# Hybrid decoder step on one core: in the u stage POOL makes the low part of the next u block before it asks for expert rows

## The chip, the core and the metric

The kernel runs on one core of a Trainium2 chip. Its time is the device time of one execution in microseconds (us), the median of several runs. The core has engines that run side by side, each with a queue of its own that it works through in order: PE multiplies matrices, DVE, ACT and POOL work on vectors, and SP issues DMA transfers. ACT and POOL issue DMAs too. The engines are kept in step by semaphores alone: an engine that waits stops everything behind the wait in its own queue.

## The reference, cut to what matters

One layer of a decoder for 512 prompt tokens and 8 x 4 sample tokens, D = 1024 wide. The change lies in its last part, PEER: a mixture of 16384 experts of one neuron each.

```
hn = rms_norm(h);  y = h + peer(hn)
peer: qh = xt @ w_pq; sub = qh . sub_keys;  top-16 per half -> 256 candidates -> top-16 (8 heads)
      pre = einsum('td,thkd->thk', xt, expert_u[experts]);  act = gelu(pre)
      out = einsum('thk,thkd->td', gate * act, expert_v[experts])
```

So each token picks 8 x 16 = 128 experts, takes the dot products of its row with their rows of expert_u, and adds up their rows of expert_v with the weights gate * gelu.

## The kernel before, in words

**Two ways to the experts.** 416 of the 544 tokens (DT) go the dense way: PE multiplies all 16384 rows of expert_u and later all rows of expert_v. The other 128 tokens (NG) go the sparse way: for each of their 128 picks POOL gathers one expert row per token by an indirect DMA (128 rows of 4 KB, `fetch`, L1721), and DVE takes the dot product (`dots`, L1731) or, in the last stage, the weighted sum (`weigh`, L1883). I call the gather with index m gather m and its dot product dot m; m runs from 0 to 127 for expert_u, and goes on from 128 for expert_v.

**The u stage.** expert_u is worked in 128 blocks of 128 experts; x counts pairs and s is 0 or 1, so block n = 2x + s, and I call the turn of the loop for (x, s) place n. A block goes through four engines: SP loads it (L1661), ACT rounds it to the high part u_hi (L1686) when PE is done with the block two before it, POOL subtracts to get the low part u_lo (`lo_u`, L1706), PE makes 24 matmuls with the two parts (`pre`, helper lines L2241 to L2243), ACT applies Gelu (L1702) and SP stores the result. u_hi and u_lo have two buffers each.

**What DVE does meanwhile.** First routing: for five groups of tokens it finds the top 16s (L1476 to L1544), 12 or 16 blocks of PE work beside each group (`WINDOW`), and PE turns each group's picks (L1308, L1313). Then the gate part: 104 quads of 4 tokens; for each, DVE builds one-hot matrices (L1558, L1561; at most 4 quads ahead, `HOT`), PE multiplies them (L1337), ACT copies them out (L1415). 13 quads make a gate block, and PE's four blocks of `pre` are cut into halves and spread between them. In both parts the dots stand inside DVE's code at fixed points: up to 13 in each routing group from the second on, 46 in the gate part, after every second quad. DVE waits there for the gathered rows.

**What sets the order around the change.** The tables `FETCH_X` say which gathers are asked for at which place; in the gate part they run two gathers ahead of the dots (`FETCH_LEAD`). In a routing group 13 gathers are spread over the places, at most one at most places. The gathered rows have 3 buffers in routing and 5 later, and `fetch` waits for the dot that frees its buffer. POOL's queue holds gathers and `lo_u` in one order, written by the loop in `pool_ffn`. `lo_u` for block n+1 waits for ACT's u_hi of that block, so for PE's end of block n-1. After the u stage comes the dense v stage, in which DVE, PE and POOL work on 128 blocks of expert_v (`lo_v` is L1911, DVE's product of gates and activations L1867, its low part L1873); its first two `lo_v` stand inside the last places of the u loop.

Of the kernel before, what the change touches and what calls it, by code (L numbers as in the profile page):

```python
# [167 lines left out]
def hybrid_step(nc, x_p, x_s, kc, vc, conv_state, s0, nmix, win, wg8, qkw, convw, alog, dtb, dnw, wout, nffn,  # L168
                wpq, skt, eu, eu_rows, ev, pos_t, lnc_p, lnc_s, squares,
                y_p, y_s, k_p, v_p, conv_out, s_p, k_s, v_s, s_s, gates_dram, acts_dram):  # L170
    with ExitStack() as ctx:
# [990 lines left out]
        def pool_sample(pool, chain):  # L1162
            pool_ffn(pool, chain)
# [26 lines left out]
        def raw(k):  # L1190
            return w_first if k == NW1 else w_raw[k % 2]
# [376 lines left out]
        def pool_ffn(pool, chain):  # L1568
            pool.wait_ge(kv_out, 16 * (NKV + 2))
            for k in range(NW1, NW3):  # L1570
                pool.wait_ge(w_hi_ready, k + 1)
                pool.wait_ge(w_used, k - 1)
                nc.gpsimd.tensor_tensor(out=w_lo[:, k % 2], in0=raw(k)[:], in1=w_hi[:, k % 2].bitcast(F32),
                                        op=ALU.subtract).then_inc(w_lo_ready, 1)
            pool.sem_inc(ff["gate_mm"], HOT)
            for s in range(2):
                pool.sem_inc(gate_out[s], 16)
                pool.sem_inc(act_out[s], 16)
            lo_u(pool, 0, 0)
            for x in range(XS):  # L1580
                for s in range(2):
                    for m in FETCH_X[2 * x + s]:
                        fetch(pool, m)
                    if s == 0 or x + 1 < XS:
                        lo_u(pool, x + s, 1 - s)
                if x in (FIRST_V, FIRST_V + 1):
                    lo_v(pool, x - FIRST_V)
            pool_dense(pool)
# [28 lines left out]
        XS = PK // 2  # L1617
# [86 lines left out]
        def lo_u(pool, x, s):  # L1704
            pool.wait_ge(dn["uhi"], 2 * x + (s + 1))
            nc.gpsimd.tensor_tensor(out=u_lo[s][:], in0=u_raw[2 * (x % 2) + s][:], in1=u_hi[s][:].bitcast(F32), op=ALU.subtract).then_inc(dn["ulo"], 1)  # L1706

        def fetch(pool, m):

            if m == 0:  # L1710
                few_wait(pool, "idx", 1)
            if m == DOT0[NT]:
                pool.wait_ge(ff["sub"], 4 * (NT - 1) + 1)
            last = ROW_LAST[m]
            if last is not None and last < PICKS:
                few_wait(pool, "dot", last + 1)
            elif last is not None:
                few_wait(pool, "sum", last - PICKS + 1)
            table = eu_rows if m < PICKS else ev.rearrange("a b d -> (a b) d")
            n = m % PICKS  # L1720
            nc.gpsimd.indirect_dma_start(out=rows_g[ROW_AT[m]][0:NG, :], out_offset=None, in_=table,  # L1721
                                         in_offset=bass.IndirectOffsetOnAxis(ap=idx_g[0:NG, n:n + 1], axis=0)).then_inc(row_in[ROW_AT[m]], 16)
# [186 lines left out]
        def lo_v(pool, f):  # L1909
            pool.wait_ge(dn["vhi"], f + 1)  # L1910
            nc.gpsimd.tensor_tensor(out=v_lo[f % 4][:], in0=v_raw[f % 4][:], in1=v_hi[f % 4][:].bitcast(F32),  # L1911
                                    op=ALU.subtract).then_inc(dn["vlo"], 1)

        def pool_dense(pool):
            for n in range(FETCH_LEAD):
                for m in FETCH_V[n]:
                    fetch(pool, m)
            for f in range(2, PK):
                for m in FETCH_V[f - 2 + FETCH_LEAD] if f - 2 + FETCH_LEAD < len(FETCH_V) else ():
                    fetch(pool, m)  # L1920
                lo_v(pool, f)
# [475 lines left out]
```

## Time and profile before

| | us |
|---|---|
| median of 3 runs (lowest, highest) | 2228.98 (2225.56, 2231.54) |
| the profiled execution, its own time | 2227.2 |
| its span, first to last instruction | 2225.4 |
| PE busy | 2014.9 (91%) |
| DVE busy | 1540.5 (69%) |
| POOL busy | 1158.6 (52%) |
| ACT busy | 771.4 (35%) |

Times in the profile run from the start of the span. The u stage runs from about 850 to 1635 us: routing to 1222, gates to 1480, then blocks without gates. The v stage runs from there to about 2216. Idle time of an engine is shown in square brackets behind the instruction that ended it, with what released it. The granted clock of PE is 0.955 of full speed in the mean.

### The profile page before, as it was taken

To read this page: it belongs to the slowest core of one execution; us is meant where nothing else is said; L and a number is where in the kernel's file an instruction comes from. 1 tells how busy PE (TensorE), PEld (TensorE's weight loads), DVE (VectorE), ACT (ScalarE), POOL (GpSimd) and SP (SyncE) were. 2 spreads that over 40 slices of the span, in tenths; PEclk is the share of its full clock that TensorE was granted. 3 is DMA by queue.
4 is the path that set the end of the run, shared out by engine and by line. 5 is a ranking of instruction groups with operands and counts; after the bars stand their busy time and mean duration, and the time that the engine had idled before them with its cause. 6 is when DMAs were issued, how large, how long until landed. Compare 5 with 4: busy or idle time off the path is not lost.

```text
span 2225.4 us, 34386 instructions
## 1 busy us (share of the span) xinstructions
PE 2014.9 (91%) x12706; PEld 1898.6 (85%) x12706; DVE 1540.5 (69%) x2782; ACT 771.4 (35%) x1228; POOL 1158.6 (52%) x632
## 2 busy tenths in 40 slices
PE   5999899787768997999898999999899999999998
PEld 5989855576658896988888998999799999999998
DVE  2377555434251105689985999964489999999996
ACT  3224144323212323444344444433323333333332
POOL 2235100123032232567576444458788888888884
PEclk9999799998759898999999999999999999999999
DMA  5664365343422354577678687789888989899894
GB/s 185 221 239 163 137 191 175 110 184 150 161 98 85 131 233 158 167 238 231 212 241 264 239 304 253 303 323 384 303 311 318 311 310 328 308 317 313 308 324 135
DMA packets 176595, 520.94 MB, mean 234 GB/s; under 512 B 15152, under 2 KB 86064, under 8 KB 170704
## 3 DMA queue, kind: packets, MB, share of 16 engines
q1 hardware_dynamic: 136560, 290.94, 37.5%
q0 software_dynamic: 36864, 134.23, 17.9%
q10 hardware_dynamic: 3056, 94.24, 10.8%
q8 instruction: 70, 1.15, 0.2%
q14 instruction: 45, 0.37, 0.1%
HBM read 456.81 MB, written 128.49 MB: 263 GB/s over the span
## 4 chain that ended last, share of the span: by engine, by line
PE 45%; DVE 35%; issue 7%; POOL 5%; ACT 4%; DMA 4%; SPq 0%; ACTq 0%; DVEq 0%; PEldq 0%; POOLq 0%
DVE acc_g L1883 10%; DVE act_l L1867 10%; PE bank L2241 8%; PE bank L2242 7%; PE bank L2243 7%; POOL u_lo L1706 3%; DVE one L1561 3%; PE twin L2241 2%; PE twin L2243 2%; PE twin L2242 2%; DMA rows_g<-eu_rows,idx_g 2%; DVE rows_g L1731 2%; PE bank L1337 2%; DVE one L1558 1%; ACT u_hi L1686 1%
## 5 line engine op out<-in xcount | busy, mean ns | idle before, releaser
L1706 POOL TENSOR_TENSOR u_lo<-u_raw,u_hi 128x1024 fp32r<-128x1024 f32 x128 | 315.7, 2466 | 296.5 <-ACT u_hi L1686 295.7
L2241 PE MATMUL bank<-hn_hi,u_hi 128*128 128x416 f32 x1024 | 374.9, 366 | 37.0 <-POOL u_lo L1706 34.3
L1911 POOL TENSOR_TENSOR v_lo<-v_raw,v_hi 128x1024 fp32r<-128x1024 f32 x128 | 335.6, 2623 | 68.8 <-ACT v_hi L1836 67.4
L2242 PE MATMUL bank<-hn_lo,u_hi 128*128 128x416 f32 x1024 | 363.9, 355 | 0.0
L2243 PE MATMUL bank<-hn_hi,u_lo 128*128 128x416 f32 x1024 | 362.4, 354 | 0.0
L1883 DVE SCALAR_TENSOR_TENSOR acc_g<-rows_g,coef,acc_g 128x1024 f32<-128x1024 f32 x127 | 292.8, 2305 | 17.0 <-DMA rows_g<-ev,idx_g 16.7
L2242 PE MATMUL bank<-a_lo,v_hi 128*128 128x416 f32 x768 | 269.2, 350 | 0.0
L2241 PE MATMUL bank<-a_hi,v_hi 128*128 128x416 f32 x768 | 269.1, 350 | 0.0
L2243 PE MATMUL bank<-a_hi,v_lo 128*128 128x416 f32 x768 | 269.0, 350 | 0.0
L2241 PEld LDWEIGHTS bank<-hn_hi,u_hi 128*128 128x128 f32 x1024 | 196.3, 192 | 52.7 <-POOL u_lo L1706 47.9
L1867 DVE TENSOR_TENSOR act_l<-act_l,gin 128x416 f32<-128x416 f32 x128 | 229.6, 1794 | 0.1
L1731 DVE CUSTOM_DVE_ANT_0 rows_g<-rows_g,twin 128x1024 f32<-128x1024 f32 x128 | 155.5, 1215 | 100.9 <-DMA rows_g<-eu_rows,idx_g 100.3
L1838 ACT ACTIVATE a_hi<-act_l 128x416 fp32r<-128x416 f32 x128 | 70.7, 552 | 379.7 <-DVE act_l L1867 379.7
L2243 PEld LDWEIGHTS bank<-hn_hi,u_lo 128*128 128x128 f32 x1024 | 195.4, 191 | 2.5
L2242 PEld LDWEIGHTS bank<-hn_lo,u_hi 128*128 128x128 f32 x1024 | 195.6, 191 | 1.0
L1721 POOL DMA_INDIRECT rows_g<-ev,idx_g x128 | 183.2, 1431 | 21.2 <-issue 16.5
L1702 ACT ACTIVATE act_c<-bank 128x416 f32<-128x416 f32 x128 | 66.2, 517 | 352.3 <-PE bank L2243 344.5
L2243 PEld LDWEIGHTS bank<-a_hi,v_lo 128*128 128x128 f32 x768 | 144.2, 188 | 1.1
L2241 PEld LDWEIGHTS bank<-a_hi,v_hi 128*128 128x128 f32 x768 | 144.2, 188 | 1.1
L2242 PEld LDWEIGHTS bank<-a_lo,v_hi 128*128 128x128 f32 x768 | 144.1, 188 | 1.1
L1721 POOL DMA_INDIRECT rows_g<-eu_rows,idx_g x128 | 128.9, 1007 | 26.0 <-issue 15.0
L1561 DVE TENSOR_SCALAR one<-bank,picks_t 128x128 f32<-128x128 f32 x416 | 141.2, 401 | 0.0
(414 smaller groups left out, 4466.5 us busy)
## 6 DMA issues: line engine op xcount, KB each, us to landing
u_raw<-eu SPq DMA_DIRECT2D x128, 512.0 KB, 5.0
v_raw<-ev SPq DMA_DIRECT2D x128, 512.0 KB, 4.6
k_s<-kc ACTq DMA_DIRECT2D x29, 1104.0 KB
v_s<-vc ACTq DMA_DIRECT2D x29, 1104.0 KB
acts_dram<-act_c SPq DMA_DIRECT2D x128, 208.0 KB, 4.2
gates_dram<-gst ACTq DMA_DIRECT2D x8, 3328.0 KB, 12.4
gin<-gates_dram SPq DMA_DIRECT2D x32, 832.0 KB, 8.6
act_l<-acts_dram SPq DMA_DIRECT2D x64, 416.0 KB, 5.8
```

Source lines behind the costliest of these rows:

```text
L1561: last = ts(one1[n % HOT][:, j, :], asc_p, picks_t[:, 0, c:c + 1], picks_t[:, 2, c:c + 1], ALU.is_equal, ALU.mult)
L1702: nc.scalar.activation(act_c[s][:], bank[s][:, 0:DT], ACT.Gelu).then_inc(dn["gelu"], 1)
L1706: nc.gpsimd.tensor_tensor(out=u_lo[s][:], in0=u_raw[2 * (x % 2) + s][:], in1=u_hi[s][:].bitcast(F32), op=ALU.subtract).then_inc(dn["ulo"], 1)
L1721: nc.gpsimd.indirect_dma_start(out=rows_g[ROW_AT[m]][0:NG, :], out_offset=None, in_=table, in_offset=bass.IndirectOffsetOnAxis(ap=idx_g[0: ...
L1731: nc.vector.tensor_tensor_reduce(out=row, in0=row, in1=x_held[0:NG, :], scale=1.0, scalar=0.0, op0=ALU.mult, op1=ALU.add, accum_out=pre_g[ ...
L1838: nc.scalar.activation(a_hi[q % 4][:], act_l[q // 2 % 2][:, q % 2, :], ACT.Copy).then_inc(dn["ahi"], 1)
L1867: tt(out=a.rearrange("p (b t) -> p b t", b=GBLOCKS), in0=a.rearrange("p (b t) -> p b t", b=GBLOCKS), in1=gin[f // 4 % 2][:, :, f % 4, :], ...
L1883: nc.vector.scalar_tensor_tensor(out=acc_g[0:NG], in0=rows_g[ROW_AT[m]][0:NG, :], scalar=coef[0:NG, n:n + 1], in1=acc_g[0:NG] if n else xg ...
L1911: nc.gpsimd.tensor_tensor(out=v_lo[f % 4][:], in0=v_raw[f % 4][:], in1=v_hi[f % 4][:].bitcast(F32), op=ALU.subtract).then_inc(dn["vlo"], 1)
L2241: nc.tensor.matmul(out, ah, bh, start=first and i == 0, stop=False)
L2242: nc.tensor.matmul(out, ah, bl, start=False, stop=False)
L2243: last = nc.tensor.matmul(out, al, bh, start=False, stop=final and i == n - 1)
```

## The change

In each place of the u loop POOL now makes the low part of the next block first and asks for its gathers afterwards. The same instructions are issued, with the same waits; only their order in POOL's queue is another.

```
             for x in range(XS):
                 for s in range(2):
+                    if s == 0 or x + 1 < XS:
+                        lo_u(pool, x + s, 1 - s)
                     for m in FETCH_X[2 * x + s]:
                         fetch(pool, m)
-                    if s == 0 or x + 1 < XS:
-                        lo_u(pool, x + s, 1 - s)
                 if x in (FIRST_V, FIRST_V + 1):
                     lo_v(pool, x - FIRST_V)
```

POOL's queue at the end of routing and the start of the gate part, before. `rows_g_...` are the buffers of gathered rows; the gathers into 192 and 175 are gathers 50 and 51, those into 193, 194 and 175 are gathers 52, 53 and 54.

```order
L1721 DMA rows_g_192<-eu_rows,idx_g 128x1024
L1721 DMA rows_g_175<-eu_rows,idx_g 128x1024
L1706 TENSOR_TENSOR u_lo_187<-u_raw_183,u_hi_185 128x1024
L1721 DMA rows_g_193<-eu_rows,idx_g 128x1024
L1721 DMA rows_g_194<-eu_rows,idx_g 128x1024
L1721 DMA rows_g_175<-eu_rows,idx_g 128x1024
L1706 TENSOR_TENSOR u_lo_188<-u_raw_184,u_hi_186 128x1024
```

The same gathers in the changed kernel.

```order
L1706 TENSOR_TENSOR u_lo_187<-u_raw_183,u_hi_185 128x1024
L1721 DMA rows_g_192<-eu_rows,idx_g 128x1024
L1721 DMA rows_g_175<-eu_rows,idx_g 128x1024
L1706 TENSOR_TENSOR u_lo_188<-u_raw_184,u_hi_186 128x1024
L1721 DMA rows_g_193<-eu_rows,idx_g 128x1024
L1721 DMA rows_g_194<-eu_rows,idx_g 128x1024
L1721 DMA rows_g_175<-eu_rows,idx_g 128x1024
```

Each gather has moved behind one more u_lo, and so behind that u_lo's wait for ACT.

POOL's queue at the end of the u stage, where gathers of expert_v and the first `lo_v` stand between the last blocks, before.

```order
L1706 TENSOR_TENSOR u_lo_187<-u_raw_190,u_hi_185 128x1024
L1911 TENSOR_TENSOR v_lo_201<-v_raw_195,v_hi_197 128x1024
L1721 DMA rows_g_175<-ev,idx_g 128x1024
L1721 DMA rows_g_176<-ev,idx_g 128x1024
L1706 TENSOR_TENSOR u_lo_188<-u_raw_191,u_hi_186 128x1024
L1721 DMA rows_g_192<-ev,idx_g 128x1024
L1721 DMA rows_g_193<-ev,idx_g 128x1024
L1706 TENSOR_TENSOR u_lo_187<-u_raw_183,u_hi_185 128x1024
```

The same stretch in the changed kernel.

```order
L1706 TENSOR_TENSOR u_lo_187<-u_raw_190,u_hi_185 128x1024
L1721 DMA rows_g_193<-ev,idx_g 128x1024
L1721 DMA rows_g_194<-ev,idx_g 128x1024
L1911 TENSOR_TENSOR v_lo_201<-v_raw_195,v_hi_197 128x1024
L1706 TENSOR_TENSOR u_lo_188<-u_raw_191,u_hi_186 128x1024
L1721 DMA rows_g_175<-ev,idx_g 128x1024
L1721 DMA rows_g_176<-ev,idx_g 128x1024
L1706 TENSOR_TENSOR u_lo_187<-u_raw_183,u_hi_185 128x1024
```

The u_lo behind `v_lo_201` no longer has two gathers ahead of it; two others now stand ahead of `v_lo_201`.

## Rows read from the trace of the kernel before

**Rows 1.** Page, part 5: busy, mean ns; idle before, releaser

```profile
L1731 DVE CUSTOM_DVE_ANT_0 rows_g<-rows_g,twin 128x1024 f32<-128x1024 f32 x128 | 155.5, 1215 | 100.9 <-DMA rows_g<-eu_rows,idx_g 100.3
L1721 POOL DMA_INDIRECT rows_g<-eu_rows,idx_g x128 | 128.9, 1007 | 26.0 <-issue 15.0
```

**Rows 2.** Stretches: length, busy PE, PEld, DVE, ACT, POOL; clock, DMA share, GB/s

```profile
925.00:1222.00 297.00, 268.68 (x1426) 259.06 (x1425) 247.17 (x799) 130.93 (x156) 199.74 (x110) 0.99 0.72 232
1222.00:1480.00 258.00, 244.37 (x1616) 240.33 (x1617) 249.91 (x622) 112.28 (x170) 119.71 (x78) 0.98 0.75 279
...
1577.00:1636.00 59.00, 46.86 (x215) 44.41 (x214) 33.38 (x23) 16.34 (x24) 47.93 (x28) 0.88 0.78 272
1636.00:2216.00 580.00, 578.23 (x3055) 568.69 (x3054) 561.30 (x367) 188.89 (x253) 486.85 (x235) 1.00 0.87 302
```

**Rows 3.** Waits of PE, 845 to 1640: us in total, times, longest

```profile
PE bank L2241 <- POOL u_lo L1706: 34.3, 26, 4.9
...
PE bank L1337 <- DVE one L1561: 9.1, 10, 2.6
```

**Rows 4.** Timeline of POOL, gather 9: start, us, instruction [idle before, releaser]

```profile
983.74 0.95 POOL L1721 DMA_INDIRECT rows_g<-eu_rows,idx_g  x1
987.13 2.43 POOL L1706 TENSOR_TENSOR u_lo<-u_raw,u_hi 128x1024 fp32r<-128x1024 f32 x1 [2.44 <-ACT u_hi L1686]
```

**Rows 5.** Timeline of DVE: dots 9 and 14, picks of the fourth group

```profile
988.87 1.22 DVE L1731 CUSTOM_DVE_ANT_0 rows_g<-rows_g,twin 128x1024 f32<-128x1024 f32 x1 [0.42 <-DMA rows_g<-eu_rows,idx_g]
...
1020.85 1.22 DVE L1731 CUSTOM_DVE_ANT_0 rows_g<-rows_g,twin 128x1024 f32<-128x1024 f32 x1 [0.72 <-DMA rows_g<-eu_rows,idx_g]
...
1161.82 0.97 DVE L1544 TENSOR_TENSOR picks<-bv,gsum 128x128 f32<-128x128 f32 x1
```

**Rows 6.** Timeline of PE: turning the picks of groups 3, 4, 5

```profile
1085.06 0.90 PE L1313 MATMUL bank<-sq,picks 128*128 128x128 f32 x3 [4.12 <-DVE picks L1544]
...
1168.90 0.49 PE L1313 MATMUL bank<-sq,picks 128*128 128x128 f32 x3
...
1222.61 0.55 PE L1308 MATMUL bank<-sq,picks 128*32 128x32 f32 x24 [5.45 <-DVE picks L1544]
```

**Rows 7.** Timeline of POOL: gather 51, then blocks 68 and 69

```profile
1213.49 1.39 POOL L1721 DMA_INDIRECT rows_g<-eu_rows,idx_g  x1 [0.30 <-issue]
1214.90 2.40 POOL L1706 TENSOR_TENSOR u_lo<-u_raw,u_hi 128x1024 fp32r<-128x1024 f32 x1
...
1231.39 2.45 POOL L1706 TENSOR_TENSOR u_lo<-u_raw,u_hi 128x1024 fp32r<-128x1024 f32 x1 [8.15 <-ACT u_hi L1686]
```

**Rows 8.** Timeline of DVE: dots 51 and 52

```profile
1220.80 1.22 DVE L1731 CUSTOM_DVE_ANT_0 rows_g<-rows_g,twin 128x1024 f32<-128x1024 f32 x1 [1.08 <-DMA rows_g<-eu_rows,idx_g]
...
1235.01 1.21 DVE L1731 CUSTOM_DVE_ANT_0 rows_g<-rows_g,twin 128x1024 f32<-128x1024 f32 x1
```

**Rows 9.** The gathered rows, gates (1222 to 1480): from issue to landing

```profile
DMA to landing us min/median/max: 4.1/6.0/14.5
```

**Rows 10.** Timeline of POOL: u_lo behind gathers 78 and 97

```profile
1367.20 2.36 POOL L1706 TENSOR_TENSOR u_lo<-u_raw,u_hi 128x1024 fp32r<-128x1024 f32 x1 [8.27 <-ACT u_hi L1686]
...
1470.73 2.39 POOL L1706 TENSOR_TENSOR u_lo<-u_raw,u_hi 128x1024 fp32r<-128x1024 f32 x1 [7.30 <-ACT u_hi L1686]
```

**Rows 11.** Timeline of DVE: dots 78, 83 and 97

```profile
1370.62 1.21 DVE L1731 CUSTOM_DVE_ANT_0 rows_g<-rows_g,twin 128x1024 f32<-128x1024 f32 x1
...
1400.87 1.22 DVE L1731 CUSTOM_DVE_ANT_0 rows_g<-rows_g,twin 128x1024 f32<-128x1024 f32 x1 [3.85 <-DMA rows_g<-eu_rows,idx_g]
...
1474.53 1.21 DVE L1731 CUSTOM_DVE_ANT_0 rows_g<-rows_g,twin 128x1024 f32<-128x1024 f32 x1
```

**Rows 12.** Stretch after a stall of PE of 2.67 us, columns as rows 2

```profile
1356.00:1364.00 8.00, 6.39 (x32) 6.31 (x33) 7.54 (x20) 2.17 (x3) 2.82 (x2) 0.79 0.99 407
```

**Rows 13.** Timeline of PE: start of block 123

```profile
1597.78 0.71 PE L2241 MATMUL bank<-hn_hi,u_hi 128*128 128x416 f32 x1 [4.94 <-POOL u_lo L1706]
```

**Rows 14.** Timeline of DVE: the last weighed row before the v stage

```profile
1630.12 1.28 DVE L1883 SCALAR_TENSOR_TENSOR acc_g<-rows_g,coef,acc_g 128x1024 f32<-128x1024 f32 x1 [2.19 <-DMA rows_g<-ev,idx_g]
```

More of the change, by code:

```diff
@@ L1581, in pool_ffn @@
                 for s in range(2):
+                    if s == 0 or x + 1 < XS:
+                        lo_u(pool, x + s, 1 - s)
                     for m in FETCH_X[2 * x + s]:
                         fetch(pool, m)
-                    if s == 0 or x + 1 < XS:
-                        lo_u(pool, x + s, 1 - s)
                 if x in (FIRST_V, FIRST_V + 1):
```

## The prediction

> **What bounds the kernel now.** I read the page's table of costly groups first. DVE stands idle 100.3 us ahead of its 128 dots, waiting for gathered rows, while POOL's gathers hardly wait at all [rows 1]: the rows come late, not POOL. Then I cut the span into stretches. In routing DVE is busy 247 of 297 us and PE 269; in the gate part DVE 250 of 258 and PE 244; in the v stage both are full [rows 2]. So in the gate part nothing has slack: a late dot delays the one-hot matrices behind it in DVE's queue, and PE waits for these, which it already does ten times [rows 3]. The waits of PE for u_lo, 34.3 us, look like what the change is after. But they are 26 waits, 1.3 us in the mean, and going through them in the timeline I find POOL itself idle ahead of most of these u_lo, waiting for ACT's u_hi, as it is 2.44 us ahead of the u_lo that follows gather 9 [rows 4]; no gather delayed them. Only in the last 60 us do gathers hold up u_lo for long, 4.94 us at block 123 [rows 13].
>
> **What the change does.** It adds and removes no instruction. Before, the gathers of place n were asked for right after u_lo of block n; now they stand behind u_lo of block n+1, which waits for u_hi, and so for PE's end of block n-1. So every gather is one block later: about 4.5 us in routing, about 7 us in the gate part. The u_lo come earlier only where a gather really held POOL. I take each gather's new issue as the end of the u_lo that now precedes it plus 0.15 us, and its landing as long after issue as before.
>
> **Routing (+10.5 us).** Gather 9 was issued at 983.74 and its dot started 5.13 us later, having waited 0.42. The next u_lo ends at 987.13 + 2.43 = 989.56 [rows 4], so the gather goes out at 989.71 and the dot starts at 994.84 instead of 988.87: 5.97 us late [rows 5]. Dots 10 to 13 had their rows early enough to add nothing. At dot 14 the 0.72 us that were waited before come off: DVE is 5.25 us late [rows 5]. Up to the picks of the third group no dot waits again, and for these picks PE already waits 4.12 us [rows 6]: PE loses 5.25 us. With PE, ACT and POOL are 5.25 us later, and the game begins anew: rows 30 to 48 were awaited before, and each now comes a block later still. The fourth group's picks come 6 us later against PE's new time; before they were ready at 1162.8, PE turned them at 1168.9 [rows 5, 6], so this is just hidden. For the fifth group, gathers 50 and 51 now follow the u_lo that ends at 1217.30; 51 is the second, at 1218.70, and with its 7.31 us of before it lands at 1226.0 instead of 1220.8: 5.2 us [rows 7, 8]. PE already waits 5.45 us for these picks [rows 6], so this is lost too. 5.25 + 5.2 = 10.5. Bounds: 0, if only the rows' landing shortens by as much, and 13, if the fourth group shows.
>
> **Gate part (+36 us).** A landing takes 6.0 us in the median here [rows 9]. Gather 52 now waits for u_lo 69, which ACT lets start only after the second quad: 1231.39 + 2.45 + 0.15 = 1233.99, landing 1240.0; its dot was at 1235.01 [rows 7, 8]: 5.0 us. After that the gathers run so far ahead that 7 us less is still enough, and two dots lose 0.3 each. But the lead melts, since DVE eats 6 rows in a gate block and the four places of one ask for 46/8 = 5.75. From gather 78 on it is too short. First: u_lo ends at 1369.56, issue 1369.71, landing 1375.7, dot at 1370.62: 5.1, of which 0.3 are in the lateness already. Last: gather 97, u_lo ends at 1473.12, issue 1473.27, landing 1479.3, dot at 1474.53: 4.7 [rows 10, 11]. Between them I went through the rows in the same way, with DVE's own lateness and PE's carried along; eleven of the twenty are late, by 4.8, 3.3, 2.1, 5.6 (gathers 78, 79, 82, 85) and 2.1, 2.7, 4.7, 0.5, 1.6, 3.2, 4.7 (88, 89, 91, 92, 94, 95, 97), together 35.3. Off come the waits of before that are now covered: 3.85 at dot 83 [rows 11] and 1.3 at dots 89 and 95. 5.0 + 0.6 + 35.3 - 5.1 = 35.8. They add up rather than overlap, because it is a circle: dot, one-hot matrices, PE's quad, PE's next half block, u_hi, u_lo, gather, dot. When a row makes DVE late, PE and POOL become late with it and the next gathers too. Bounds: with the shortest landing, 4.1 us [rows 9], the same sum is 20; with 8 us it is 56.
>
> **PE's clock (+4 us).** After a stall of 2.67 us the granted clock over 8 us was 0.79, so PE worked part of them at 1.2 instead of 2.4 GHz: 0.21 x 8 = 1.7 us [rows 12]. The change makes some seven stalls of 3 to 5 us. At 1.7 each that is 12; but where DVE is the late one, a slower PE partly fills the stall. I take 4, bounds 0 and 12.
>
> **The end of the u stage (-2 us).** Block 123's u_lo no longer has two gathers ahead of it: at 1.0 us [rows 1] and a gap of 0.3 [rows 7] each that is 2.6 of PE's 4.94 us [rows 13], and as much at block 125, whose u_lo stands likewise behind a v_lo. PE would end the u stage some 5 us earlier. But POOL is busy 48 of 59 us there without the gaps between its gathers [rows 2], and the v stage starts with DVE, whose last early row waits for its gather still [rows 14]. That gather is behind the same work as before. In the v stage DVE is busy 561 of 580 us [rows 2], so its start counts, not PE's. I take 2 of the 5, bounds 0 and 6.
>
> **The sum.** 10.5 + 35.8 + 4 - 2 = 48. The profiled execution took 2227.2 us, 1.8 below the median of 2228.98; 2227.2 + 48 + 1.8 = 2277. I say 2276.
>
> **A rule that speaks for less.** The trace has 4.1 to 14.5 us from issue to landing of a gather, 6.0 in the median [rows 9]. The Trainium skill (DMA: Bandwidth & Descriptors, Anatomy of one DMA) gives a fixed 2.0 us plus bytes over 436 GB/s, by which these 512 KB would land in 3.2 us. By that, an estimate, the gate part would lose about 14 instead of 36. The trace does not agree: not one gather in that part landed in under 4.1, beside the gate writes and expert blocks that share the DMA engines.
>
> **Rivals.** (a) The gate part is milder: the rows whose dots come late land in 4 to 5 us, since a gather that is asked for later is asked for after the gate block's write and not during it. For it speaks that row 83 took 14.5 us beside such a write and others 4.1; against it, that the median is 6.0 [rows 9]. Price: 10.5 + 20 - 2 + 1 = 29, so 2258. The Trainium skill's rule above would lead here, and a little lower. (b) It is faster. The mechanism is POOL at places 120 to 126: the stalls at blocks 123 and 125 each start PE at half clock (the stretch has a clock of 0.88 [rows 2]), and if DVE follows PE there, 6 to 9 us come back. It decides only if the rows in routing and gates were early enough, a shift of a block costing under 6 us there. Against it speaks the plain reading of DVE's 100.3 us [rows 1]. It would give 2222. (c) The order doesn't matter: POOL is busy 120 of 258 us in the gate part [rows 2] and the gathers' place hides in its idle time. That would be so if DVE had slack, as it has after 1480. It would give 2229.
>
> **Chances.** (Main) 0.64, from 2258 to 2300 with its bounds. (a) 0.26. (b) 0.05. (c) 0.05. A measurement of this kernel tells 0.3%, 6.7 us, from no change. Main and (a) are both slower: 0.90; same 0.05, faster 0.05. The range leaves out (b), (c), the lowest part of (a) and the highest of main: 2246 to 2300.
>
> **What would show it.** In the changed trace DVE's idle time ahead of its dots should rise from 100 us to 150 or more in spite of the kernel's being longer by less; PE's waits for one-hot matrices from 9.1 to 35 or more, longest 4 to 5; the waits for the third and fifth group's picks to 9 and 10 us; each gather should follow a u_lo that before came after it, with leads in the last gate blocks of 6 us, all of it landing time. The wait at block 123 should shrink to 1 to 3. If the gate part from the fifth group's picks to the last quad is not longer than 275 us against about 257, the circle is not there and I am wrong; if the v stage starts as much earlier against the last quad as PE gained, my cap by DVE at the end is wrong.

## The result, and the profile after

| | before | after |
|---|---|---|
| median (lowest to highest), 4 runs each on one chip | 2230.26 (2225.56 to 2234.06) | 2291.82 (2290.23 to 2296.7) |
| the profiled execution, its own time | 2227.2 | 2292.2 |
| its span | 2225.4 | 2290.4 |

The ratio is 1.0281, 95% interval 1.0255 to 1.0306: slower by some 62 us. I had said 2276 with a range from 2246 to 2300, so the side and the range held, and the loss was 14 us larger than the 48 that I had added up.

The page's costly groups show the same 128 dots of the same length with 173 us of waiting for rows ahead of them, 100.3 before [rows 1] (busy, mean ns; idle before, releaser):

```profile
L1731 DVE CUSTOM_DVE_ANT_0 rows_g<-rows_g,twin 128x1024 f32<-128x1024 f32 x128 | 155.5, 1215 | 173.4 <-DMA rows_g<-eu_rows,idx_g 173.0
```

PE's waits in the u stage (us in total, times, longest). The one for the one-hot matrices is five times that of [rows 3]; the one for u_lo, which the new order was to help, fell by 3.3 us:

```profile
PE bank L1337 <- DVE one L1561: 45.8, 17, 7.0
PE bank L2241 <- POOL u_lo L1706: 31.0, 23, 3.2
...
PE bank L1308 <- DVE picks L1544: 9.5, 1, 9.5
PE bank L1313 <- DVE picks L1544: 6.6, 2, 4.6
```

The stretches of after, for routing (from the first group's picks), the gate part, the blocks at the end of the u stage and the v stage; columns as in [rows 2]:

```profile
927.65:1237.12 309.47, 274.25 (x1426) 264.83 (x1425) 241.53 (x799) 130.93 (x156) 195.78 (x108) 0.96 0.68 223
1237.73:1543.31 305.58, 257.48 (x1617) 250.96 (x1618) 248.87 (x615) 112.25 (x170) 121.72 (x80) 0.92 0.64 233
1640.00:1697.00 57.00, 48.50 (x229) 46.07 (x228) 35.55 (x20) 15.20 (x22) 49.60 (x29) 0.91 0.83 280
1697.00:2281.00 584.00, 582.02 (x3050) 568.13 (x3049) 562.68 (x369) 190.29 (x255) 486.42 (x235) 1.00 0.86 301
```

The same stretch of the gate part in before, from the fifth group's picks to the end of the last quad's copy:

```profile
1222.61:1480.09 257.48, 244.46 (x1617) 240.42 (x1618) 249.42 (x617) 112.37 (x170) 119.49 (x78) 0.98 0.75 279
```

The work is the same, DVE is busy as long, and the stretch is 48.1 us longer. PE's share of it has two parts: 35.1 us more idle (48.1 against 13.0) and 13.0 us more busy, at a clock of 0.92 instead of 0.98.

For all kernels I cut the profiled span at three marks: the first group's picks (DVE, L1544, gate_w), the turning of the fifth group's picks (PE, L1308) and the last quad's copy (ACT, L1415). The instructions ahead of the first mark are the same everywhere. `c2_again` is `c2_route1` once more. In us:

| | start of first group's picks | routing | gate part | the rest |
|---|---|---|---|---|
| before | 924.1 | 298.6 | 256.9 | 745.9 |
| after | 926.7 | 311.0 | 305.0 | 747.7 |
| e1_routing | 923.8 | 312.6 | 258.8 | 745.0 |
| e2_gates | 931.2 | 295.1 | 302.7 | 747.4 |
| e3_end | 925.6 | 297.1 | 258.8 | 745.3 |
| e4_lead4 | 929.7 | 312.5 | 253.4 | 750.5 |
| e8_new_lead3 | 928.1 | 312.1 | 268.9 | 749.2 |
| e5_half_old | 928.5 | 295.8 | 250.4 | 746.8 |
| e6_half_new | 926.2 | 310.4 | 283.9 | 748.0 |
| e7_new_leads | 928.2 | 295.8 | 256.4 | 748.6 |
| c1_lead3 | 926.3 | 298.7 | 251.3 | 745.9 |
| c2_route1 | 921.6 | 290.2 | 251.4 | 746.9 |
| c3_lead4 | 931.3 | 290.1 | 253.6 | 746.2 |
| c2_again | 929.3 | 288.6 | 250.5 | 745.6 |

So of the 65.0 us between the two spans 12.4 lie in routing, 48.1 in the gate part, 1.8 behind it, and 2.6 ahead of all that the change touches.

### The profile page after: what moved, and what is told of

Its sections match the earlier page's. It is cut to its first block, busy times and chain, and to the rows that moved or that the text cites. A ratio compares the mean times of both kernels' runs of the same rounds, so it can differ in the third digit from the quotient of the medians.

```text
span 2290.4 us, 34386 instructions
## 1 busy us (share of the span) xinstructions
PE 2039.7 (89%) x12706; PEld 1916.1 (84%) x12706; DVE 1539.3 (67%) x2782; ACT 771.3 (34%) x1228; POOL 1156.0 (50%) x632
## 4 chain that ended last, share of the span: by engine, by line
PE 41%; DVE 31%; DMA 9%; issue 7%; POOL 6%; ACT 4%; SPq 0%; ACTq 0%; DVEq 0%; PEldq 0%; POOLq 0%
DVE acc_g L1883 10%; DVE act_l L1867 9%; PE bank L2241 6%; PE bank L2242 6%; PE bank L2243 6%; DMA rows_g<-eu_rows,idx_g 6%; POOL u_lo L1706 4%; PE bank L1337 2%; PE twin L2241 2%; PE twin L2243 2%; PE twin L2242 2%; DVE rows_g L1731 1%; ACT u_hi L1686 1%; DMA w_raw<-wpq 1%; PE bank L883 1%
## 5 line engine op out<-in xcount | busy, mean ns | idle before, releaser
L2241 PE MATMUL bank<-hn_hi,u_hi 128*128 128x416 f32 x1024 | 380.9, 372 | 32.9 <-POOL u_lo L1706 31.0
L2242 PE MATMUL bank<-hn_lo,u_hi 128*128 128x416 f32 x1024 | 369.4, 361 | 0.0
L2243 PE MATMUL bank<-hn_hi,u_lo 128*128 128x416 f32 x1024 | 367.3, 359 | 0.0
L2241 PEld LDWEIGHTS bank<-hn_hi,u_hi 128*128 128x128 f32 x1024 | 201.0, 196 | 48.4 <-POOL u_lo L1706 44.3
L1337 PE MATMUL bank<-one,one 128*128 128x128 f32 x832 | 114.0, 289 | 46.6 <-DVE one L1561 45.8
L1337 PEld LDWEIGHTS bank<-one,one 128*128 128x128 f32 x832 | 109.5, 202 | 50.9 <-DVE one L1561 49.6
## 6 DMA issues: line engine op xcount, KB each, us to landing
gates_dram<-gst ACTq DMA_DIRECT2D x8, 3328.0 KB, 11.8
```

Source lines behind the costliest of these rows:

```text
L1337: last = nc.tensor.matmul(quad(4 + n % 2)[:, j, :], one2[n % HOT][:, j, :], one1[n % HOT][:, j, :], start=True, stop=True)
L2241: nc.tensor.matmul(out, ah, bh, start=first and i == 0, stop=False)
L2242: nc.tensor.matmul(out, ah, bl, start=False, stop=False)
L2243: last = nc.tensor.matmul(out, al, bh, start=False, stop=final and i == n - 1)
```

## The experiments

**The change in three parts.** e1_routing, e2_gates and e3_end use the new order in one part of the u loop each and the old one elsewhere:

```
+                    low_first = <the part>       # e1: x < GATE_X0; e2: GATE_X0 <= x < LAST_X0; e3: x >= FIRST_V
+                    if low_first and (s == 0 or x + 1 < XS):
+                        lo_u(pool, x + s, 1 - s)
                     for m in FETCH_X[2 * x + s]:
                         fetch(pool, m)
-                    if s == 0 or x + 1 < XS:
+                    if not low_first and (s == 0 or x + 1 < XS):
```

> The new order in the routing part alone (places 0 to 67), the old order after it. Theory L (every gather is one block later, DVE's dots wait, and PE waits for DVE): the traces of before and after differ by 12.5 us between the first group's picks and the fifth's, so this kernel should be 12 us slower than before (9 to 15), with PE waiting 9 to 10 us for the fifth group's picks and the gate part as long as before. Rival G (the cost lies only in the gate part and what routing lost is an accident of one execution, or the later gathers collide with the loads of the next u block everywhere): 0 to 4 us slower.

Measured: 2243.77 us (before, run beside this kernel, the next two and e4_lead4: 2230.27), ratio 1.0067 (1.0045 to 1.0089). That is 13.5 us by the medians and 15 by the ratio; the profile puts 14.0 into routing. PE waits 9.4 us for the fifth group's picks, and the gate part is 1.9 us longer than before.

> The new order in the gate part alone (places 68 to 99). Theory L: the traces differ by 48.1 us from the fifth group's picks to the last copy of a gate quad; so 48 us slower than before (42 to 53), PE's waits for one-hot matrices about 45 us, routing as before. Rival S (the parts do not add up, since DVE comes into the gate part with a deficit from routing and pays it there): under 40 us, or PE's waits for the one-hot matrices under 35.

Measured: 2277.53 us, ratio 1.0217 (1.0184 to 1.0250), 48 us by the ratio. PE's waits for the one-hot matrices are 42.4 us, 18 times, and the gate part is 302.7 us long, 45.8 us more than before.

> The new order only from place 120 on, where gathers of expert_v and the first two low parts of v stand between the last u blocks. My step at the end (DVE's start into the v stage is what counts, PE's gain is cut off): between 2 us faster and 2 us slower than before, with PE's last Gelu some 3 us earlier. Rival P (PE's gain of 3 to 5 us goes through): 3 to 5 us faster. Rival W (the last weighed rows come later and DVE enters the v stage late): 2 to 5 us slower, as the trace of after has it.

Measured: 2228.41 us, ratio 0.9997 (0.9983 to 1.0010): no difference. The three ratios add up to 62.6 us, the whole change is 62.7. The intervals of the three are 3 to 7 us wide on either side, so what is shown is that the parts lean on each other by no more than some 10 us; places 100 to 119 keep the old order in all three. The gate part has three quarters of the loss.

**The same order with more lead.** e4_lead4 and e8_new_lead3 are the changed kernel with the gathers of the gate part four and three ahead of the dots instead of two (`FETCH_LEAD`). The edit of e4_lead4, its line cut short; e8_new_lead3 has a 3 for the 4:

```
-            upto = min(FETCH_X[n][-1] + 1 + (FETCH_LEAD if n < 2 * LAST_X0 or first >= PICKS else 1), ...
+            upto = min(FETCH_X[n][-1] + 1 + (4 if n < 2 * LAST_X0 else FETCH_LEAD if first >= PICKS else 1), ...
```

> The changed kernel with the gathers of the gate part asked for 4 rows ahead of the dots instead of 2; places give 1.44 rows each, so this more than takes back the one place that the new order costs there. Theory L: the gate part is about as long as before the change (257 us instead of 305), so the kernel is 12 to 18 us slower than before and 45 us faster than the changed one. Rival C (the new order costs by what the gathers collide with in the DMA engines or by POOL's queue, not by their lead): it stays 40 us or more slower than before.

Measured: 2243.12 us, ratio 1.0055 (1.0035 to 1.0075). The gate part is 253.4 us, shorter than before the change. In the waits of PE the one-hot matrices have fallen from 45.8 us to:

```profile
PE bank L1308 <- DVE picks L1544: 10.5, 1, 10.5
PE bank L1313 <- DVE picks L1544: 10.3, 2, 6.2
PE bank L1337 <- DVE one L1561: 6.9, 10, 2.6
```

What is left is the routing part, where this kernel is as the changed one. For the gate part this is the run that decides between the lateness of rows and any price of the new order on POOL itself: POOL's queue has the same subtracts first in every place, and the whole loss of the gate part is gone.

> The changed kernel with a lead of three gathers in the gate part instead of two; the routing part as in the change. It stands between after (2291.8) and e4_lead4 (2243.1). Theory L, by the waits of the changed kernel: one more gather of lead gives a row most of one dot's place in DVE's order (some 5 us) more time, while PE's longest wait for a one-hot was 7.0 us, so 35 to 48 of the 48 us come back: 2243 to 2256 us. Rival (each step of lead gives half): about 2267 us.

Measured: 2261.27 us (before: 2229.23), ratio 1.0146 (1.0118 to 1.0173), between my two cases. The gate part is 268.9 us: 36 of its 48 us are back with the first gather of lead and the other 12, and 3 more, with the second. I had thought one would do, because I had not counted with landings of 14 us (below): of the 13.4 us that DVE still waits for rows in this part, 10.4 are for four rows asked for beside the write of a gate block, one of which took 14.7 us to land.

**The same order with shorter landings.** e5_half_old and e6_half_new fetch half a row (512 columns) in the gate part, in the old and in the new order; dots, queue and lead are as in before and after. They leave out the other half of the data, so what they compute is not the layer. Gathers 52 and 53, the first into their buffers, stay whole. The edit, its lines cut short:

```
+            half = DOT0[NT] <= m < DOT0[NT + 1] and ROW_USE[m] > 0
+            w = D // 2 if half else D
-            ...(out=rows_g[ROW_AT[m]][0:NG, :], out_offset=None, in_=table,
+            ...(out=rows_g[ROW_AT[m]][0:NG, 0:w], out_offset=None, in_=table.rearrange("a (h d) -> (a h) d", h=2) if half else table,
```

> The order of before, but the gathers of the gate part (all but the first fill of each buffer there) fetch 512 columns of a row instead of 1024, half the bytes; DVE's dots stay as long as they were (they read the other half of the buffer as it stands, so the dots' values are not the reference's). It is the base for e6_half_new. Theory L (what counts in the gate part is when a row lands against when its dot wants it): the old order has the rows asked for early enough, so little is to be had: PE's waits for the one-hot's product of 9.1 us could shrink by a few, 2224 to 2231 us. A rival by which the gathers' traffic itself slows the gate part (the DMA share is 0.65 there) would make this kernel 10 us or more faster, under 2220.

Measured: 2223.4 us (before, run beside this kernel, the next, c1_lead3 and c2_route1: 2232.14), ratio 0.9966 (0.9946 to 0.9986). That is 8 us faster by the ratio, 0.6 us under my range and not the 10 or more of the rival; the gate part is 6.5 us shorter. (The DMA share of that part in before is 0.75 [rows 2], not the 0.65 that I wrote.)

> The changed kernel (new order everywhere) with the same halved gathers in the gate part. Only the landing time of a row is shortened (about 5.7 us median there now; I expect 3.5 to 4.5), the order on POOL is that of the change. Theory L: each late row is late by that much less, so of the 48 us that the gate part lost some 15 to 25 come back: 2265 to 2278 us, and PE's waits for the one-hot's product fall from 45.8 us to 20 to 30. Rival C (the loss is in POOL's order itself, the subtract ahead of the gathers and the turns that it costs, whatever the rows take to land): as e5_half_old plus 61 us, 2285 to 2293.

Measured: 2271.95 us, ratio 1.0201 (1.0164 to 1.0237). The change costs 33.5 us in the gate part here (283.9 against 250.4) where it costs 48.1 with whole rows. From issue to landing of a gather, and PE's wait, in e6_half_new:

```profile
DMA to landing us min/median/max: 3.2/4.2/13.4
```

```profile
PE bank L1337 <- DVE one L1561: 28.8, 19, 4.8
```

In after:

```profile
DMA to landing us min/median/max: 4.1/5.7/14.6
```

So 1.5 us less in the median landing goes with 17 us less in PE's waits for the one-hot matrices, about 1 us from each, with POOL's queue untouched. Half the bytes took a quarter off the median landing, and less than a third of the gate part's loss went: 14.6 of 48.1 us.

**Lead everywhere.** e7_new_leads is the new order with lead four in the gate part and one gather more of lead in routing; c3_lead4 (below) is the old order with the same leads.

```
-        first = FETCH_X[2 * GATE_X0 - 1][-1] + 1
+        first = 0
+        for n in range(2 * WINDOW[0] + 1, 2 * GATE_X0):
+            upto = min(FETCH_X[n][-1] + 2, DOT0[NT]) if FETCH_X[n] else first
+            FETCH_X[n] = list(range(first, max(first, upto)))
+            first = max(first, upto)
```

> The new order everywhere, with the rows asked for earlier everywhere: one gather more of lead in the routing part, a lead of four gathers in the gate part. Theory L: nothing of the loss is left, and the time lies at that of c2_route1 (2213.5 us) or up to 12 us above it (PE's waits for picks and one-hot as there), 2212 to 2226 us. Rival O (the subtract ahead of the gathers has a price of its own, which the lead only covers in part): the routing part keeps the 12 us of e4_lead4 whatever is asked earlier, 2234 to 2245 us.

Measured: 2232.58 us, ratio 1.0015 (0.9998 to 1.0032). Both theories missed, the first by 7 us and the second by 1. The profile says why the first was too bold: routing is 295.8 us, 16 less than with the new order alone, but 5.7 more than in c3_lead4, and PE still waits 6.9 us for the fifth group's picks, where c3_lead4 has 2.8. One gather of lead makes up for most of a block of delay, not for all of it; more lead in routing was not tried. Of the 18.9 us between its span and c2_route1's, by which I had set the range, 6.6 lie ahead of the first mark and so say nothing of the order.

**Versions that might beat both.** c1_lead3: the old order up to the last places, lead three in the gate part. c2_route1: that, and the routing lead of the diff above. c3_lead4: c2_route1 with lead four.

> A version that might beat before: the old order up to block 123, a lead of three gathers instead of two in the gate part, and the new order only in the last places (x from FIRST_V). Theory L: PE's 9.1 us of waits for the one-hot's product and DVE's three row waits (dots 83, 89, 95 and their like) in the gate part go, at most 2.6 us of it were on a path, and the end of the u stage gives back 0 to 2: 2224 to 2230 us. Rival: the third buffer of lead takes its slot from the gather after, POOL waits longer for a dot before it makes u_lo, and PE's waits for u_lo grow by some us: 2231 to 2238.

Measured: 2224.45 us (before: 2232.14), ratio 0.9974 (0.9957 to 0.9991), within my range. The gate part is 5.6 us shorter than in before.

> c1_lead3 with one gather of lead in the routing part too (each place asks for its row one gather earlier, up to the last of the routing's). Theory L: PE's waits for the third and the fifth routing group's picks (4.12 and 5.45 us before) shrink to 0 to 2 each, so 5 to 9 us below c1_lead3: 2216 to 2224 us. Rival: only three buffers are there in routing, so POOL waits in a gather for a dot with u_lo behind it and PE waits for u_lo instead: no gain or some us lost, 2226 to 2240.

Measured: 2213.53 us, ratio 0.9933 (0.9907 to 0.9958), 2.5 us below my range. In its waits PE has none left for the third group's picks and half of the fifth's:

```profile
PE bank L2248 <- POOL u_lo L1713: 28.6, 28, 3.2
...
PE bank L1337 <- DVE one L1561: 4.8, 5, 2.9
PE bank L1308 <- DVE picks L1544: 2.8, 1, 2.8
```

The rival, that u_lo would suffer from the earlier gathers, is not there: 28.6 us against 30.5 in c1_lead3, and 32.1 when the kernel was run once more (c2_again), which is still less than the 34.3 of before.

> c2_route1 with a lead of four gathers in the gate part instead of three, the pair of e7_new_leads in the old order. Theory L: PE's waits for the one-hot's product are down to 4.8 us already, so no difference from c2_route1 beyond 2 us: 2211 to 2216 us. Rival: all buffers are filled, POOL waits for the dots with u_lo behind it, and it is 3 to 10 us slower than c2_route1.

Measured: 2220.76 us (before: 2229.23), ratio 0.9960 (0.9943 to 0.9976). That is 5 us above my range, where the rival had it, and it has the rival's symptom. POOL waits for dots to free a buffer, which it did for only 1.8 us in c2_route1:

```profile
POOL rows_g L1728 <- DVE pre_g L1738: 44.5, 23, 3.9
```

But against c2_route1 the gate part is only 2.2 us longer, and PE's waits for u_lo, 30.6 us, lie between the 28.6 and 32.1 of the two runs of c2_route1. Of the 11.1 us between the two profiled spans 9.7 lie ahead of the first mark, where both kernels are the same, so I ran c2_route1 again:

> c2_route1 once more, word for word, with runs of before beside it: c3_lead4, which differs from it in the gate part alone, came out 7 us above it, and in the two profiles 9.7 of 11.1 us lay ahead of the first routing group's picks, where no kernel here differs. If c2_route1's gain is real, its time is 2210 to 2221 us again and the ratio's interval stays under 1. If that call was lucky, it lies with c3_lead4 at 2219 to 2225 us.

Measured: 2215.73 us (before: 2228.57), ratio 0.9949 (0.9931 to 0.9967). The gain of c2_route1 is real, 11 to 15 us by its two ratios, and it beats both kernels. Behind the first mark c3_lead4 took 1.4 us longer than c2_route1 and 5.3 longer than c2_again, 3.1 of these in the gate part. So the fourth gather of lead gains nothing, and how much it costs stays open.

## Why the prediction was right, and where it was too small

**Routing, +10.5 predicted, +12.4 in the profile, 13.5 to 15 alone in e1_routing.** Gather 9 goes out behind the next u_lo, as I said, and its dot waits. In after, POOL and then DVE:

```profile
990.08 2.43 POOL L1706 TENSOR_TENSOR u_lo<-u_raw,u_hi 128x1024 fp32r<-128x1024 f32 x1 [2.44 <-ACT u_hi L1686]
992.65 0.95 POOL L1721 DMA_INDIRECT rows_g<-eu_rows,idx_g  x1
```

```profile
991.46 1.22 DVE L1731 CUSTOM_DVE_ANT_0 rows_g<-rows_g,twin 128x1024 f32<-128x1024 f32 x1 [4.89 <-DMA rows_g<-eu_rows,idx_g]
997.79 1.22 DVE L1731 CUSTOM_DVE_ANT_0 rows_g<-rows_g,twin 128x1024 f32<-128x1024 f32 x1 [1.93 <-DMA rows_g<-eu_rows,idx_g]
```

Less the 2.65 us by which this execution starts later, dot 9 is 6.27 us late against [rows 5]; I had 5.97. The delays then show on PE where it turns the picks:

```profile
1092.80 0.79 PE L1313 MATMUL bank<-sq,picks 128*128 128x128 f32 x3 [4.63 <-DVE picks L1544]
...
1179.86 0.55 PE L1313 MATMUL bank<-sq,picks 128*128 128x128 f32 x3 [1.93 <-DVE picks L1544]
...
1237.73 0.55 PE L1308 MATMUL bank<-sq,picks 128*32 128x32 f32 x24 [9.53 <-DVE picks L1544]
```

Against [rows 6] and less the same 2.65, PE is 5.1 us late at the third group, 8.3 at the fourth, 12.5 at the fifth. I had 5.25, 5.25 and 10.5. The fourth group is the step that failed: I had called it "just hidden", and it shows with 3.2 us, as PE's wait there does in four more kernels with this order in routing (4.1 us each in e1_routing, e4_lead4, e6_half_new and e8_new_lead3). It was the upper bound that I had named ("13, if the fourth group shows"). My sign for the third group was wrong as well: the wait there did not go to 9 us but to 4.63, from 4.12; for the fifth I had 10, and it is 9.53. From the first mark to the third group's turn PE was busy 4.25 us longer in after for the same 804 matmuls, at a granted clock of 0.97 instead of 1.00:

```profile
924.05:1085.06 161.01, 145.85 (x804) 140.48 (x804) 142.10 (x475) 73.66 (x89) 109.22 (x60) 1.00 0.70 228
```

```profile
926.70:1092.80 166.10, 150.10 (x804) 144.58 (x804) 140.74 (x475) 73.66 (x89) 107.12 (x59) 0.97 0.68 222
```

So most of the 5.1 us shows as slower matmuls and not as a longer wait. A wait that doesn't grow is no sign that nothing was lost in front of it. That 5.1 is so near my 5.25 is in part luck. In e6_half_new, where PE lost nothing to its clock up to there (145.8 us busy, clock 1.00), the wait grew by 2 us and PE was 2.5 us late; in e1_routing, e4_lead4 and e8_new_lead3 it was 3.8 to 4.0 us late. By these runs the late rows alone cost less at the third group than I had said, and the fourth group made up for it.

**Gate part, 36 us predicted for the rows and 4 for the clock; 48.1 measured.** The circle is there: DVE's row waits in this part, from dot 52 to dot 97, add up to 54.1 us in twelve waits; less the 5.1 of before that went (dots 83, 89 and 95, the first in [rows 11]) that is 49.0, which is all of the 48.1. Predicted were 40.9 less 5.1. I had taken 6.0 us for every landing, and the late rows are of two kinds, one on either side of it. Five of the twelve (dots 52, 79, 85, 91, 97) landed in 4.2 to 6.1 us from their issue, four quicker than I took and one as I took it; they waited 22.0 us, where I had 23.3. The first of them, POOL and DVE:

```profile
1249.08 0.95 POOL L1721 DMA_INDIRECT rows_g<-eu_rows,idx_g  x1
```

```profile
1253.38 1.22 DVE L1731 CUSTOM_DVE_ANT_0 rows_g<-rows_g,twin 128x1024 f32<-128x1024 f32 x1 [3.18 <-DMA rows_g<-eu_rows,idx_g]
```

That is 3.18 us late instead of 5.0. The other seven (59, 65, 70, 76, 82, 88, 94) took 8.4 to 14.6 us and waited 32.1, where I had some 6, and they have one thing in common: they were asked for beside the write of a finished gate block, 3.3 MB from ACT's queue. Gather 70 on POOL, the write on ACT's queue, dot 70 on DVE:

```profile
1341.54 0.94 POOL L1721 DMA_INDIRECT rows_g<-eu_rows,idx_g  x1 [0.31 <-issue]
```

```profile
1341.68 0.34 ACTq L1422 DMA_DIRECT2D gates_dram<-gst  x1
```

```profile
1356.17 1.22 DVE L1731 CUSTOM_DVE_ANT_0 rows_g<-rows_g,twin 128x1024 f32<-128x1024 f32 x1 [5.23 <-DMA rows_g<-eu_rows,idx_g]
```

Gather 76 goes out 0.17 us ahead of the next write and takes 14.5 us. The other five go out 5.8 to 5.9 us behind one and take 8.4 to 10.5. Each of the first seven writes of the gate part has one of the seven. It is the same for the rows that made nobody wait: of the 92 gathers of the gate part in before and after, the 24 that went out between 0.2 us ahead of a write and 7.3 us behind its start took 8.1 to 14.6 us, the other 68 took 4.1 to 8.2. That the write is the cause is read from this; a kernel with the write moved or left out was not tried. In before such landings did little harm, 3.85 us at dot 83 [rows 11] and 1.3 at dots 89 and 95, since the lead covered the rest; with a block less of lead the first comes through at dot 59, where I had allowed 0.6 us for all rows up to 77 and 14.8 were lost (dots 59, 65, 70, 76). That is the mis-sized term: the step "after that the gathers run so far ahead that 7 us less is still enough" took the lead against the median landing and not against the slowest that comes once in every gate block. From gather 78 on I had 35.3 and measured 36.2, and that these agree is luck. Seven dots were late there and not eleven: 78, 89, 92 and 95, for which I had 11.2 us, did not wait at all, and the seven waited 36.2 us where I had 24.1 for them, most of the difference again at the rows beside a write (82, 88 and 94: 17.4 instead of 5.8). PE's longest wait for a one-hot matrix, where I had named 4 to 5 us, became 7.0, right behind dot 94.

In this part nothing is to be had from the clock as a term of its own. PE lost 13.0 us to it, three times my 4, but they lie within the circle: a slower quad is a later u_hi, a later gather and a longer wait of DVE, which the 49 us already hold. That is argued from the trace; no run held the clock apart.

On the landing of a gather, the Trainium skill (DMA: Bandwidth & Descriptors, Anatomy of one DMA) has 2.0 us plus bytes over 436 GB/s, by which 512 KB take an estimated 3.2 us. That stays under every landing in the gate part of after too, where the shortest was 4.1 and the median 5.7.

**Rival (a),** the milder gate part, asked whether late gathers land sooner because they are asked for behind the write and not during it. Half of it was right: the five above that were not beside a write did, four of them in 4.2 to 4.9 us. But 5.8 us behind the start of a write that takes 11.8 us in the median is not behind it, and two went out right with one. e6_half_new gives it its due: where the landings are shorter, the loss is 33.5 us.

**The end of the u stage, -2 predicted, +1.8 in the profile, no difference alone in e3_end.** The stalls shrank, 4.94 us [rows 13] to 2.97, and 4.80 to 3.21 at block 125:

```profile
1660.58 0.71 PE L2241 MATMUL bank<-hn_hi,u_hi 128*128 128x416 f32 x1 [2.97 <-POOL u_lo L1706]
...
1675.76 0.46 PE L2241 MATMUL bank<-hn_hi,u_hi 128*128 128x416 f32 x1 [3.21 <-POOL u_lo L1706]
```

The last Gelu comes 3.1 us earlier after the last quad than before (149.2 against 152.3 us). DVE's first a_lo of the v stage comes 2.5 us later (156.7 against 154.3): the gathers of the early expert_v rows now stand behind the u_lo, and DVE waits for them, here at one of the first and at the last:

```profile
1653.74 1.29 DVE L1883 SCALAR_TENSOR_TENSOR acc_g<-rows_g,coef,acc_g 128x1024 f32<-128x1024 f32 x1 [6.68 <-DMA rows_g<-ev,idx_g]
...
1694.46 3.87 DVE L1883 SCALAR_TENSOR_TENSOR acc_g<-rows_g,coef,acc_g 128x1024 f32<-128x1024 f32 x2 [3.30 <-DMA rows_g<-ev,idx_g]
...
1699.45 0.59 DVE L1873 TENSOR_TENSOR a_lo<-act_l,a_hi 128x416 fp32r<-128x416 f32 x1 [0.62 <-ACT a_hi L1838]
```

So the cap by DVE that I had named was the right mechanism, and "that gather is behind the same work as before" was wrong. e3_end shows what the order at the end is worth by itself: its last Gelu comes 3.9 us earlier after the last quad than in before, and from PE's first matmul of the v stage on it takes 3.3 us longer (597.2 us against 593.9), so this part is 0.6 us shorter in all. after has 598.8 there, at a granted clock of 0.995. The old order has 1.6 us more than before in one execution too (e5_half_old: 595.5, clock 0.995), so about that much of the +1.8 may be the execution and not the order; this was not tried apart. Rival (b), the faster one, dies with it: PE's gain at the end is real and reaches nobody. Rival (c), that the order does not matter, falls by e1_routing and e2_gates; with enough lead it is nearly true, as e4_lead4 shows for the gate part.

**The sum.** Predicted 10.5 + 35.8 + 4 - 2 = 48; in the profile 12.4 + 48.1 + 1.8 = 62.3. Missing were 1.9 in routing (3.2 for the fourth group, less 1.0 at the fifth), 8 in the gate part and 4 at the end. The 8 are themselves a difference: 14.2 too little for dots 59 to 76 and 0.9 from gather 78 on, against 1.8 too much for dot 52 and the 4 of the clock, which is no term of its own, and some 1 us that DVE waited and the stretch did not lose. So the side, the mechanism of the circle and the range were earned, and the size came out as near as it did with some luck.

## What to carry to other kernels

When two engines are held in a circle by a queue's order, price a moved request by the slowest landing that recurs in it, not by the median, and look at what big transfer starts at a fixed beat beside it. A request for data should not stand behind work that waits for the end of the block before. Asking earlier, by one gather in routing and two in the gate part, gave back here what the order cost (e7_new_leads); in the old order, asking one gather earlier in both parts gained 11 to 15 us (c2_route1, which has the new order in the last places, worth nothing by itself). A gain at a stall is only worth what the engine that starts the next stage takes of it.

## What the runs showed of the hardware that I had not expected

A gather of 512 KB landed in 4.1 us at best and took 14.6 when it went out 0.14 us ahead of a write of 3.3 MB on another queue: its order of issue did not protect it. Halving the bytes of such gathers took the median only from 5.7 to 4.2 us, and the longest from 14.6 to 13.4, beside writes of the same size.

The stretch ahead of the first group's picks has the same instructions in every kernel here, and ends between 921.6 and 931.3 us. Between the two ends of this range the granted clock from 200 to 400 us differs. First c2_route1 (921.6), then c3_lead4 (931.3):

```profile
200.00:400.00 200.00, 182.40 (x1571) 140.55 (x1570) 114.39 (x334) 77.41 (x207) 24.73 (x33) 0.94 0.49 162
```

```profile
200.00:400.00 200.00, 182.81 (x1555) 140.35 (x1554) 114.12 (x330) 74.20 (x200) 25.69 (x33) 0.91 0.48 158
```

Over all the kernels the two go together only loosely (c1_lead3 has 926.3 at a clock of 0.915, e7_new_leads 928.2 at 0.940), and PE's busy time in the stretch is nearly the same, so what makes the start longer stays open. A few us between two profiles of this kernel mean nothing until both are counted from the same mark.
